# Seven products instead of eight for sixteen of the 22 feature tiles of the second down projection

## The reference, cut to what matters

```python
hn = rmsnorm(h, pre_ffn_norm[i])
ff = (jax.nn.silu(hn @ w_gate[i]) * (hn @ w_up[i])) @ w_down[i]   # [512, 2816] @ [2816, 1024]
h = h + rmsnorm(ff, post_ffn_norm[i])
e = rmsnorm(p[i] @ w_ple_proj[i], ple_norm[i])
gate = jax.nn.sigmoid(h @ w_ple_gate[i] + b_ple_gate[i])
h = h + e * gate
```

## Time and profile before

| | before |
|---|---|
| median of 3 runs | 1527.83 us (1526.61 to 1528.1) |
| profiled execution, span from first to last instruction | 1525.5 us |
| TensorE busy | 1511.5 us, 99% |
| VectorE busy | 1136.2 us, 74% |
| ScalarE busy | 799.4 us, 52% |
| GpSimd busy | 149.6 us, 10% |
| mean granted TensorE clock | 0.999 |

### The profile page before, as it was taken

The page is one execution under the profiler, slowest core; times in us unless marked ns, Lnnn a source line. Parts: engine busy times, 40 slices in busy tenths (PEclk is TensorE's granted clock), DMA queues, the critical chain, the costliest instruction groups (busy, mean ns, idle before and its releaser), DMA issues.

```text
span 1525.5 us, 21551 instructions
## 1 busy us (share of the span) xinstructions
PE 1511.5 (99%) x8214; PEld 1290.1 (85%) x8214; DVE 1136.2 (74%) x1844; ACT 799.4 (52%) x1284; POOL 149.6 (10%) x158
## 2 busy tenths in 40 slices
PE   8999999999999999999999999999999999999998
PEld 3788877878888899999888888788888999988887
DVE  8999988897898789977664547766577888843356
ACT  5545467764553656666442335446355666643233
POOL 0111000000000101111011011110202111100100
PEclk9999999999999999999999999999999999999999
DMA  9778221223566547666633323211234566573241
GB/s 370 184 187 202 83 90 62 88 86 108 210 230 211 165 117 190 197 162 166 184 100 103 111 86 100 75 49 42 97 116 147 147 165 164 145 250 101 87 138 69
DMA packets 66632, 213.05 MB, mean 140 GB/s; under 512 B 7773, under 2 KB 10077, under 8 KB 65506
## 3 DMA queue, kind: packets, MB, share of 16 engines
q1 hardware_dynamic: 52784, 178.63, 34.3%
q0 software_dynamic: 13744, 33.04, 11.2%
q10 hardware_dynamic: 2, 0.00, 0.0%
HBM read 175.47 MB, written 7.87 MB: 120 GB/s over the span
## 4 chain that ended last, share of the span: by engine, by line
PE 91%; DVE 4%; ACT 2%; issue 1%; DMA 1%; ACTq 0%; DVEq 0%; SPq 0%
PE bank L1940 18%; PE bank L1941 18%; PE bank L1948 18%; PE bank L1978 8%; PE bank L1988 8%; PE bank L1980 8%; PE bank L2006 2%; PE bank L2020 1%; PE bank L2018 1%; PE bank L2019 1%; PE bank L2110 1%; PE bank L2093 1%; PE bank L2123 1%; DVE tmp L2670 1%; PE bank L2137 1%
## 5 line engine op out<-in xcount | busy, mean ns | idle before, releaser
L1940 PE MATMUL bank<-HH,sph 128*128 128x512 f32 x856 | 342.9, 401 | 2.2 <-ACT xpad L2227 0.8
L1941 PE MATMUL bank<-HH,spl 128*128 128x512 f32 x856 | 333.9, 390 | 0.0
L2537 DVE TENSOR_TENSOR spl<-raw,sph 128x1024 fp32r<-128x1024 f32 (+2 forms) x166 | 205.2, 1238 | 161.4 <-ACT sph L2168 161.3
L2168 ACT ACTIVATE sph<-raw 128x1024 fp32r<-128x1024 f32 (+2 forms) x186 | 189.1, 1020 | 150.8 <-PE bank L1948 117.5
L1948 PE MATMUL bank<-HL,sph 128*128 128x512 f32 x856 | 225.5, 396 | 0.0
L1940 PEld LDWEIGHTS bank<-HH,sph 128*128 128x128 f32 x856 | 160.8, 188 | 40.1 <-issue 5.7
L1941 PEld LDWEIGHTS bank<-HH,spl 128*128 128x128 f32 x856 | 160.8, 188 | 34.5 <-issue 1.4
L1948 PEld LDWEIGHTS bank<-HL,sph 128*128 128x128 f32 x856 | 159.8, 188 | 35.2 <-issue 1.9
L2599 DVE SCALAR_TENSOR_TENSOR convout<-convin,vecs,convout 128x512 f32<-128x512 f32 x240 | 166.4, 748 | 0.0
L1978 PE MATMUL bank<-HH,sph 128*128 128x256 f32 x576 | 144.7, 284 | 0.0
L1980 PE MATMUL bank<-HH,spl 128*128 128x256 f32 x576 | 144.4, 283 | 0.0
(11 more groups left out here) (366 smaller groups left out, 2686.4 us busy)
## 6 DMA issues: line engine op xcount, KB each, us to landing
raw<-in_w_in SPq DMA_DIRECT2D x69, 512.0 KB, 3.2
raw<-in_w_up SPq DMA_DIRECT2D x66, 512.0 KB, 4.5
more<-in_w_ada SPq DMA_DIRECT2D x32, 512.0 KB, 5.6
raw<-in_w_down SPq DMA_DIRECT2D x32, 512.0 KB, 3.7
raw<-in_w_gate SPq DMA_DIRECT2D x22, 512.0 KB, 3.8
raw<-raw POOLq DMA_DIRECT2D x36, 256.0 KB, 4.4
midl<-tmp POOLq DMA_DIRECT2D x36, 256.0 KB, 3.3
spl<-raw POOLq DMA_DIRECT2D x17, 512.0 KB, 5.5
```

The costliest lines, as they stand in the source:

```text
L1940: e.matmul(P_[b][:], sph(n)[:, q], hi[:, k, :], start=k == 0, stop=False)
L1941: e.matmul(P_[b][:], spl(n)[:, q], hi[:, k, :], start=False, stop=False)
L2168: e.activation(sph(n), raw(n), ACT.Copy).then_inc(*up("s_w_high", ("wh", n)))
L2537: e.tensor_tensor(spl(n), raw(n), sph(n).bitcast(F32), ALU.subtract).then_inc(*up("s_w_low", ("wl", n)))
```

## The change

Feature tiles 0 to 5 of the down projection stay plain: 8 output tiles by one unit of 128x768. For tiles 6 to 21 the output tiles are taken in four pairs, and each pair in seven products of 8 feature tiles, 128 outputs and 256 tokens, each again with high and low halves: 28 products with 24 matmuls of 256 columns. `XT` becomes the accumulator: ScalarE copies the plain result into it (`down_plain`), and after each product that completes a term VectorE adds or subtracts the bank (`down_add`, six for a pair). The sums of activations for the scheme are made from the hidden values, which are now kept whole in `MF` (`down_t_sum`, `down_t_high`, `down_t_low`, `down_x_low`); most of these are pieces of the generator `down_first` that runs beside the plain tiles. The weights' sums are made by VectorE (`down_sum`, three for a pair) and by one GpSimd DMA that adds 512 KB (`down_third`). The two interleaved steps `down_factors` and `down_settle` set the order. The plain tiles' low weight halves are made by VectorE. The squares of `ff` are summed by VectorE instead of GpSimd, the residual is read back into `FFO` late in the stage, `branch` is gone for this projection and `join` takes the gain in. `EC` is squared in place and summed by VectorE (`e_square`, `e_total`, `e_join`).

```diff
+DOWN_PLAIN = 6
+DOWN_PARTS = 28
+DOWN_FIRST = ((6, 14), (10, 18))
...
+    def down_factors(st, count, beside=None):
+        while st["made"] < min(count, st["total"]):
+            s = st["made"]
+            pos = s % 7
+            if pos in (2, 3):
+                add("down_sum", s)
+            add("down_high", s)
+            if beside:
+                beside()
+                beside = None
+            add("down_low", s)
+            st["made"] += 1
+            if pos in (2, 4, 5) or pos == 6 and s < st["total"] - 1:
+                load()
+            if pos == 6 and s < st["total"] - 1:
+                add("down_sum", s + 2)
+                add("down_third", s // 7 + 1)
+        if beside:
+            beside()
...
+    def t_sums(t):
+        for g in range(2):
+            add("down_t_sum", t, g, [label for j in range(4) for label in frees[j]] if t == 3 else [])
+        for g in range(2):
+            add("down_t_high", t, g)
+
+    def down_first():
+        t_sums(0)
+        yield
+        t_sums(1)
+        yield
+        add("down_t_low", 0, 0)
+        yield
+        add("down_t_low", 0, 1)
+        yield
+        t_sums(3)
+        yield
+        add("down_t_low", 1, 0)
+        add("down_t_low", 1, 1)
+        yield
+        for g in range(2):
+            add("down_x_low", 0, g)
+        yield
+        for g in range(2):
+            add("down_t_sum", 2, g, [])
+        yield
+        add("down_sum", 1)
+        add("down_third", 0)
+        yield
+        add("down_x_low", 2, 0)
+        yield
+        add("down_x_low", 2, 1)
+        yield
+        add("down_t_low", 3, 0)
+        yield
+        add("down_t_low", 3, 1)
+        yield
+        add("down_x_low", 1, 0)
+        yield
+        add("down_x_low", 1, 1)
...
+    load()
+    side.append(down_first())
+    rate[0] = 1
     for i in range(8):
-        gemm("w_down", i, NFT, "m2", branch("FFO", i, ssf), 2 if i == 7 else 1)
+        gemm("w_down", i, DOWN_PLAIN, "m2", plain_evac(i))
+    flush()
+    rate[0] = 0
...
+    for s in range(DOWN_PARTS):
+        if s == 1:
             add("e_copy")
             add("p_load", 2)
+            ssf = SumSq("ff")
+        down_factors(down, s + 3, lambda: down_settle(s - 1) if s else None)
+        if s:
+            down_square(s - 1)
+        W["cut"] = max(W["cut"], down["first"] + down["made"])
+        if s < 2:
+            add("down_t_high", 2, s)
+        if 1 <= s < 3:
+            add("down_t_low", 2, s - 1)
+        if s in range(8, 20, 2):
+            add("e_square", (s - 8) // 2)
+        if s in range(11, 21, 2):
+            add("e_total", (s - 9) // 2)
+        if s == 22:
+            add("p_cut", 2)
             add("root_table", keepc(1))
+        if s >= DOWN_PARTS - 2:
+            split()
+        if s in (23, 24):
+            add("x_reload", 2, s - 23)
+        add("down", s, banks[s // 7 % 2], banks[2 + s // 7 % 2])
+        done()
+    down_settle(DOWN_PARTS - 1)
+    down_square(DOWN_PARTS - 1)
...
     ready("pool", more=2)
...
+            def down(s, sums, pairs):
+                p, pos = divmod(s, 7)
+                step = step_of(s)
...
+                elif step == 2:
+                    w.wait_ge(at("down_add", p, 0))
+                elif step == 4:
+                    w.wait_ge(at("down_add", p, 1))
+                elif step == 5:
+                    w.wait_ge(at("down_add", p, 2))
+                elif step == 6:
+                    w.wait_ge(at("down_add", p, 4))
+                w.wait_ge(at("down_low", s))
...
+            def down_high(s):
+                given, after = down_given(s)
+                w.wait_ge(at(*down_free(s)), *each(after))
+                e.activation(SPH[down_slot(s)][:], given, ACT.Copy).then_inc(*up("s_w_high", ("down_high", s)))
...
+            def down_low(s):
+                w.wait_ge(at("down_high", s))
+                e.tensor_tensor(SPL[down_slot(s)][:], down_given(s)[0], SPH[down_slot(s)][:].bitcast(F32),
+                                ALU.subtract).then_inc(*up("s_w_low", ("down_low", s)))
...
             def join(name, i, b, j, free):
                 ver = {"MIXO": 4, "FFO": 5}[name]
+                if ver == 5:
+                    w.wait_ge(at("rows", "ff"), at("ff", i), *each(free))
+                    e.scalar_tensor_tensor(TMP[j][:], XT[:, i, :], vec("g_pof", i), P_[b][:], ALU.mult,
+                                           ALU.mult).then_inc(*up("s_x", ("join", name, i)))
+                    w.wait_ge(at("join", name, i), at("x_back", 2, i // 4))
+                    e.tensor_tensor(XT[:, i, :], FFO[:, i, :], TMP[j][:], ALU.add).then_inc(
+                        *up("s_x", ("x", ver, i)))
+                    return
```

More of the change, by code:

```diff
@@ L71, with whole_mid @@
 SCALE = 1.0 / float(np.sqrt(96.0))
+def whole_mid(which, f):
+    return which == 2 and f >= DOWN_PLAIN
 class Ring:
@@ L167, in split @@
             if st["first"] <= cut < st["first"] + st["slots"]:
-                factors(st, 2 * (cut - st["first"]) + 2)
+                if st["down"]:
+                    down_factors(st, cut - st["first"] + 1)
+                else:
+                    factors(st, 2 * (cut - st["first"]) + 2)
                 W["cut"] += 1
@@ L908, in pair_bank, with last @@
             return banks[2 + i % 2]
+        def last(i):
+            return ("seven", which, 7 * i + 8) if i == f1 - f0 - 2 else None
         def settle(pos, i):
+            if pos == 6:
+                return
             if pos == 0:
@@ L1474, in ffn_rows @@
             add("seven_full", 2, i)
[L1476 to L1481, removed]
     ffn_up(2, "n4", lambda i, z: (("w_gate", "w_up")[z], i), ffn_rows)
     fence("d2")
-    ssf = SumSq("ff")
-    for i in range(8):
-        if i == 1:
+    ssf = None
+    frees = dict(tmp.take() for _ in range(NT))
+    for j in range(4, NT):
+        tmp.give(j, *frees[j])
+    n_down = W["used"] + 8
+    down = {"first": n_down + sum(st["slots"] - st["units"] for st in stages), "units": 16, "slots": DOWN_PARTS,
+            "total": DOWN_PARTS, "made": 0, "down": True}
@@ new lines, in plan @@
+    stages.append(down)
+    add("down_begin", n_down, down["units"], down["slots"])
+    def t_sums(t):
[37 more added lines that the diff above has]
+        add("down_x_low", 1, 1)
@@ L1498, in plan @@
+    down_settle(DOWN_PARTS - 1)
+    down_square(DOWN_PARTS - 1)
+    for p in (2, 3):
+        main.give(banks[p % 2][0], ("down_add", p, 6))
+        main.give(banks[2 + p % 2][0], ("down_add", p, 5))
+    for j in range(4):
+        tmp.give(j, ("down", DOWN_PARTS - 1))
+    sse = SumSq("e")
     fence("er")
@@ L1819, in load @@
                 name, tile, first, size = units[n]
[L1820 to L1825, removed]
+                if n >= 2 * NRAW:
+                    w.wait_ge(*each(raw_before(n)))
+                where = f"d_extra{extras[n]}" if n in extras else f"d_raw{raw_turn(n) % NRAW}"
+                e.dma_start(raw(n), A[name][tile, :, first:first + size]).then_inc(*up(where, ("raw", n), by=16))
             def open_load(p):
```

312 lines of the change are left out of this document (262 added, 50 removed).

## The result

The kernel after takes 1532.45 us (median of 5 runs, 1531.65 to 1534.16), the one before 1527.16 in the same series (5 runs, 1526.61 to 1528.10): ratio 1.0038, interval 1.0025 to 1.0050. It is 5.3 us slower; the forecast was 1532.4 us, 4.6 more than before. The agreement within 0.1 us is luck in part: the forecast started from the 1527.8 of the first three runs, 0.6 above this series, and its difference was 0.7 too small.

What follows compares the result with a forecast made beforehand. The number and spacing of TensorE's matmuls bound the stage. Terms: +1.9 (stage -6.4 and +7.4, late add +0.9), +0.45, +2.0, 0.3 for restarts: +4.6 on 1527.8 gives 1532.4 us; range 1526.0 to 1536.5.

Steps and rivals of the forecast that it cites:

- Spacing and exchange: Projection stage: 384 matmuls of 512 columns (0.2267 us each) replaced by 672 of 256 (0.12 each), gaining 6.4 us.
- rival of half-price matmuls: Products 2 to 27: 256-column matmuls at 0.1133 us, half of 512, 4.2 us shorter, total 1528.2; chance 0.04.
- the larger gain that the Trainium skill's formula gave: Projection stage: with matmuls at 216 and 109 ns the same exchange would be worth 9.7 us; the forecast followed the trace.
- Stalls by the walk of VectorE's queue: TensorE waiting at plain tiles 3, 5, 6, products 2, 3 and the start of pairs 2 and 3: 7.4 us.
- restarts: TensorE's restarts after waits, a separate term of the sum: 0.3 us.
- Late add: Projection's end: the last add waits for VectorE's low half of the first `w_pg` unit: +0.9 us.
- Root: Behind the projection: ScalarE makes two high halves ahead of the square root, delaying it 0.45 us.
- Lock: Behind the projection: first residual sum, two SBUF operands, blocked until GpSimd's second low half ends: +2.0 us.
- DMAs: Projection stage: 512 KB adding DMAs, taken as 7 us to landing, covered by products 0 to 3: cost nothing.

Runs made afterwards that it cites:

- e1: Kernel after without most low halves of activations in the seven-product part, the third pass taking the high half again: 1527.57 us, ratio 1.0003.
- e9: Kernel after with the low halves of plain tiles 4 and 6 made by ScalarE's negative copy and an adding DMA: 1530.70 us, ratio 1.0024.
- e2: Kernel after with the add of the finished product listed ahead of the weight sum at each pair's third factor: 1534.34 us, ratio 1.0042.
- e3: Kernel after with VectorE's low half for the first w_pg unit moved behind the last add: 1531.84 us, ratio 1.0032.
- e6: Kernel after with three 512-column warm matmuls between the two groups of one-column sums: 1532.57 us, ratio 1.0031.
- e5: Kernel after with the third low half for w_pg made by VectorE behind the first join instead of by GpSimd: 1532.17 us, ratio 1.0031.
- e4: Kernel after with the low halves of plain tiles 2 to 7 made by ScalarE and an adding DMA: 1537.78 us, ratio 1.0067.
- e10: Kernel after with the edits of e3, e5 and e9 together, without warm matmuls: 1529.67 us, ratio 1.0016.
- e7: Kernel after with the edits of e3, e5 and e6 together: 1533.25 us, ratio 1.0035.
- e11: Kernel after with the edits of e3 and e5 together, without warm matmuls: 1530.93 us, ratio 1.0026.
- e8: Kernel after with the edits of e7 and e9 together: 1531.05 us, ratio 1.0024.

## Why the prediction was right

It named the place of each loss, and the runs bear out the mechanisms. w_pg's first matmul was forecast 129.9 us behind the projection's and came at 130.43. By its own steps:

- *Spacing and exchange.* The short matmuls are 0.12 apart (24 in 2.88 us) and the exchange has about its 6.4 us: e1's stage, corrected for its stops, is some 6 below the old one. The rival of half-price matmuls is out, and so is the larger gain that the Trainium skill's formula gave (TensorE: Matmul & The Clock Gate, Back-to-back issue gap): the matmuls of 512 columns stay 0.2267 apart, not 0.216.
- *Stalls by the walk of VectorE's queue.* Forecast 1.5, 0.5, 1.3, 2.1, 0.6, 0.7 and 0.7; the brackets say 1.08, 0.27, 1.05, 1.76, 0.41, 0.61 and 0.77, each with 0.26 on top. Together 8.1 against 7.4 + 0.3 for restarts. The first tile behind a wait starts at 13.52 (forecast 13.7), product 2 at 43.59 (43.8). VectorE has no gap over 2 us there; ScalarE's queue makes the longest (1.97), as the walk had it at tile 3, and a second one of 1.13 stands ahead of factor 2's low. e1 and e9 show that taking work from VectorE removes these waits, e2 that a new order doesn't.
- *Late add.* 1.1 against 0.9; e3 shows 0.6 of it to be the low half ahead of the add.
- *Root.* The square root was 0.46 later, as forecast (0.45). The spread at the lower clock added 0.33, which was not foreseen, but e6, at the full clock and with the same distance, shows it to be hidden by the next term.
- *Lock.* 1.41 in the row, forecast 2.0, mostly because the sum starts later; e5, which takes away one GpSimd operation, gave 1.88 from products' end to w_pg, which is this term and 0.47 of the root's delay that it hid; 0.33 of that is the clock, which did not fall there. The first join, with a PSUM operand, kept its 0.75 under GpSimd, and the sum with two SBUF operands waited for all of it. The Trainium skill's rule (SBUF — State Buffer, Who interferes with whom), that the later of the two blocks until the other ends, is what all seven profiles with two GpSimd operations show (after, e1, e2, e3, e4, e6, e9), with 0.54 to 0.56 us from GpSimd's end to the sum's, wherever the sum starts.
- *DMAs.* The 512 KB adding transfers landed in 4.4 us (taken as 7), as the issues on the page after say (count, KB, median us to landing), and no engine waited for one. Costing them at nothing held, though e4 shows what a wait of theirs does to whatever stands behind them in GpSimd's queue.

```profile
raw<-raw POOLq DMA_DIRECT2D x4, 512.0 KB, 4.4
```

Against the forecast the stage came out 0.4 too long (1.73 for 1.3), the add 0.2 and the root 0.3 too late, and the lock 0.6 too short. These partly cancel, and that the sum of 4.6 comes so near the 5.03 of the rows (5.3 in the medians) is in part luck.

**Open.** Why the clock falls in one execution and not in the next wasn't settled. The spread of the times (1531.65 to 1534.16 after) would fit falls inside the stage in some executions, but also the opening part, which differs by up to 2.65 us between the profiles, and is at its longest in the profile of after, whose time is the highest of its five. Only profiled executions tell. What a fall behind the stage costs e10 is read from one pair of profiles. Whether the 1.13 us in which VectorE waits for ScalarE ahead of product 2 could be filled wasn't tried. Whether moving half of the sums to another engine would let the exchange pay wasn't tried.

## What to carry to other kernels

Price an exchange of matmuls for elementwise work by walking the helper's in-order queue to each point where TensorE wants something, not by shares of busy time: here VectorE had 23 us free in the stage and TensorE still lost all of its 6.4 us. Work cut ahead for the next stage (a high half before the square root, a low half before the last add, a second GpSimd operation) is no cover where nothing else runs; place it behind the chain that ends the stage. And of two chains that end together, a change to one shows nothing while the other is longer: in the kernel after the lower clock cost nothing to w_pg (e6), in e10 it cost 0.98.

## What the runs showed of the hardware

- A stop of 1.75 to 1.88 us of TensorE ahead of product 2 or 3 was followed by a granted clock of 0.50, from 0.2 to 1.5 us after its restart, for about 3 us, in four of seven profiles (e2, e3, e5, e7; not in the kernel after, e6 and e11). It cost 0.82 us in e3, e5 and e7 (stage 122.27 to 122.28 for 121.44 to 121.46). Without such a stop (e1, e8, e9, e10) it never fell there; in e4's stop of 5.73 us it fell during the stop. The Trainium skill (TensorE: Matmul & The Clock Gate, What's actually happening) says of a kernel's start that the number of matmuls at the lower clock differs from run to run with the phase of the gate. No run here shows that for the start; that e3 fell and e11 not, with the same program up to a stop of 1.78 and 1.75 us, agrees with it.
- Behind the stage, where one-column matmuls stand around 0.4 to 1 us of idle time, it fell in seven of the nine profiles of the changed kernels without warm matmuls, in none of the three with them, and not in the kernel before.
- A stop costs TensorE 0.24 to 0.26 us more than the idle time in the profile's bracket (seven stops of the kernel after).
- Plain fp32 matmuls of 512 columns stand as two records each, 0.44 us apart (six in 2.66 us in e6), where an fp32r one takes 0.2267.
